# A hybrid attention layer pair on one core: the first query unit on the unscaled operand, r and bias applied to its results

## What is computed

```python
def rmsnorm(x, g):
    y = x * rsqrt(mean(x * x, axis=-1) + 1e-6)
    return y * g
h = rmsnorm(x, g[0])
proj = h @ w_in + b_in            # 256 x 2048 by 2048 x 2560
q, k, v = split(proj, [2048, 2304])
q = q * HEAD_DIM ** -0.5          # then 32 heads of 64; 4 heads of k and v
```

## Time and profile before

| | |
|---|---|
| median of 3 runs | 2267.7 us |
| the runs | 2261.79, 2267.7, 2271.3 us |
| the profiled execution | 2263.93 us, its span 2262.2 us |
| mean granted TensorE clock | 0.981 |
| TensorE busy | 2173.0 us, 96% of the span |
| VectorE busy | 1353.5 us, 60% |
| ScalarE busy | 1083.9 us, 48% |
| GpSimd busy | 249.2 us, 11% |

### The profile page before, as it was taken

One profiled execution on the slowest core, in us unless ns is written; L12 is line 12 of the kernel. 1 busy time (PEld: TensorE's weight loads), 2 busy tenths in 40 slices (PEclk: granted clock), 3 DMA queues, 4 the chain that ended last, 5 costly groups with the idle time before them and its releaser, 6 DMA issues.

```text
span 2262.2 us, 34176 instructions
## 1 busy us (share of the span) xinstructions
PE 2173.0 (96%) x11553; PEld 1805.5 (80%) x11553; DVE 1353.5 (60%) x2081; ACT 1083.9 (48%) x1639; POOL 249.2 (11%) x395
## 2 busy tenths in 40 slices
PE   8999989999999999998989998989999999999998
PEld 7777778888888888886776666768888888888886
DVE  7655567676767644445765444457766666664444
ACT  6766454444444443444455555445444444443443
POOL 3341000000000000003004554000000000000000
PEclk9999999999999999998999999999999999999999
DMA  6435545655565665553562222535555555665553
GB/s 211 136 116 177 177 139 170 202 182 194 174 201 178 192 208 191 186 188 110 189 222 66 74 74 81 172 129 186 187 184 193 178 195 176 197 209 189 186 187 129
DMA packets 107194, 381.12 MB, mean 168 GB/s; under 512 B 14114, under 2 KB 14578, under 8 KB 106482
## 3 DMA queue, kind: packets, MB, share of 16 engines
q1 hardware_dynamic: 104962, 373.69, 50.4%
q10 hardware_dynamic: 2160, 6.46, 0.7%
HBM read 377.97 MB, written 2.14 MB: 168 GB/s over the span
## 4 chain that ended last, share of the span: by engine, by line
PE 88%; DVE 6%; ACT 2%; issue 2%; POOL 1%; DMA 1%; DVEq 0%; ACTq 0%; POOLq 0%; SPq 0%
PE set L535 35%; PE set L603 29%; PE set L539 17%; DVE wlo L1266 2%; PE set L700 2%; PE set L682 1%; PE set L724 1%; PE set L627 1%; DVE scored L1524 1%; ACT whi L906 1%; DVE x_sb L1431 1%; POOL probs L490 1%; PE set L684 1%; DMA raw<-in_stream 0%; PE set L717 0%
## 5 line engine op out<-in xcount | busy, mean ns | idle before, releaser
L535 PE MATMUL set<-hs,whi 128*128 128x512 f32 x3584 | 1220.8, 403 | 20.4 <-DVE wlo L1266 7.6
L1266 DVE TENSOR_TENSOR wlo<-raw,whi 128x1024 fp32r<-128x1024 f32 x704 | 858.1, 1229 | 577.5 <-ACT whi L906 576.8
L906 ACT ACTIVATE whi<-raw 128x1024 fp32r<-128x1024 f32 x704 | 738.5, 1057 | 766.2 <-PE set L539 404.8
L539 PE MATMUL set<-hs,wlo 128*128 128x256 f32 x3584 | 856.2, 282 | 0.0
L539 PEld LDWEIGHTS set<-hs,wlo 128*128 128x128 f32 x3584 | 675.7, 191 | 78.6
L535 PEld LDWEIGHTS set<-hs,whi 128*128 128x128 f32 x3584 | 624.0, 191 | 119.4 <-issue 19.1
L603 PE MATMUL set<-whi,hid 128*128 128x512 f32 x1408 | 386.9, 395 | 0.0
L603 PEld LDWEIGHTS set<-whi,hid 128*128 128x128 f32 x1408 | 264.6, 188 | 63.5 <-DVE wlo L1266 0.6
L603 PE MATMUL set<-wlo,hid 128*128 128x512 f32 x704 | 222.5, 395 | 0.0
L603 PEld LDWEIGHTS set<-wlo,hid 128*128 128x128 f32 x704 | 132.4, 188 | 31.7
L603 PE MATMUL set<-whi,os 128*128 128x512 f32 x512 | 146.8, 400 | 0.0
(11 more groups left out here) (178 smaller groups left out, 1180.8 us busy)
## 6 DMA issues: line engine op xcount, KB each, us to landing
raw<-in_stream SPq DMA_DIRECT2D x704, 512.0 KB, 3.4
gain_rows<-rows ACTq DMA_DIRECT2D x4, 1024.0 KB, 5.2
xT<-in_x SPq DMA_DIRECT2D x8, 256.0 KB, 7.9
out_y<-out_f SPq DMA_DIRECT2D x3, 512.0 KB, 2.6
bo_rows<-rows ACTq DMA_DIRECT2D x1, 1024.0 KB, 7.9
wg_raw<-in_w_gates ACTq DMA_DIRECT2D x1, 768.0 KB, 4.4
out_y<-out_f SPq DMA_DIRECT2D x2, 256.0 KB, 2.4
w2k_sb<-in_w ACTq DMA_DIRECT2D x2, 128.0 KB, 5.2
```

Of the source, the lines that this page charges most:

```text
L535: return mm(sets[set_of(u)][:, t, 0:2 * w], whi[:, slot, cols], r, start=first, stop=final)
L539: return mm(sets[set_of(u)][:, t, w:2 * w], wlo[:, slot, cols], r[:, 0:w], start=False, stop=False)
L906: A(whi[:, slot, :], raw[:, slot, :], ACT.Copy).then_inc(hi_ready, 1)
L1266: V.tensor_tensor(wlo[:, slot, :], raw[:, slot, :], whi[:, slot, :].bitcast(F32), ALU.subtract).then_inc(lo_ready, 1)
```

## The change

KV0's chunks are no longer interrupted by `spread_r(0)`, which moves behind chunk 2 of Q0, uses a bank of set 1 instead of set 0 and waits for KV0's evacuation. Q0 reads the unscaled `hs`, and its results get the two-step treatment `q0_unscaled`: DVE adds the halves, DVE multiplies by r and by -1/8, ACT adds the bias. The scaling of `hs` starts in Q0's chunk loop (`scale_x(0)` at loop step c = 4, then one chunk for each step from 5 to 10) and ends behind Q0's evacuation (the low half of chunk 6, all of chunk 7). `high_of_scaled(c)` now waits for Q0's use of chunk c. The second query unit waits for all of it (`h_ready` of 16). `duplicate(0)` moves from DVE to ACT, with `ACT.Copy`. For chunk 0 of KV0, DVE makes `wlo` ahead of copying x out.

```diff
--- before.py
+++ after.py
...
@@ -632,19 +633,19 @@
                 def waits(c):
                     if c + 1 < CH:
                         turn_x(n, c + 1)
-                    if n == 0 and c == 6:
-                        spread_r(0)
                     pe.wait_ge(h_ready, h_before(n) + c + 1)
                 return waits
 
             def spread_r(n):
 
+                bank = sets[1] if n == 0 else norm_banks[n]
                 if n == 0:
                     pe.wait_ge(post_in, 32)
-                    nc.tensor.transpose(norm_banks[0][0:5 * KT, UT - 1, S:S + P], post_sb[:].rearrange("p a b -> p (a b)"),
+                    pe.wait_ge(evacuated, UT * (KV0 + 1))
+                    nc.tensor.transpose(bank[0:5 * KT, UT - 1, S:S + P], post_sb[:].rearrange("p a b -> p (a b)"),
                                         ident[:])
                 pe.wait_ge(diag_ready, n + 1)
-                mm(norm_banks[n][:, UT - 1, 0:S], ones[:], diag[:].rearrange("p a b -> p (a b)"), start=True,
+                mm(bank[:, UT - 1, 0:S], ones[:], diag[:].rearrange("p a b -> p (a b)"), start=True,
                    stop=True).then_inc(r_spread, 1)
 
             def attention(layer, u_q, g, last):
@@ -804,6 +805,8 @@
                            start=True, stop=True).then_inc(vc_rep_done, 1)
                     if layer == 1 and c == 0:
                         fold_halves(WV1)
+                    if layer == 0 and c == 2:
+                        spread_r(0)
                     if c != 5:
                         return
                     if layer == 0:
@@ -831,10 +834,6 @@
                     ins.then_inc(vc_done, 1)
                 return after
 
-            def scaled_waits(c):
-
-                pe.wait_ge(h_ready, CH + c + 1)
-
             for layer in range(2):
                 q0, o0, ff, dn = ((Q0, O0, FF0, DN0), (Q1, O1, FF1, DN1))[layer]
                 n = 2 * layer
@@ -850,13 +849,15 @@
                     unit(KW1, hs)
                     compress_unit(WK1, 0, after_wk)
                     compress_unit(WV1, 1, after_wv)
-                unit(q0, hs, waits=scaled_waits if layer == 0 else None, after_chunk=after_q0(layer))
+                unit(q0, hs, after_chunk=after_q0(layer))
                 if layer == 1:
 
                     pe.wait_ge(kc_ready, 1)
                     pe.wait_ge(vc_rep_ready, 1)
                     pe.wait_ge(gate_exp, 1)
                 pe.wait_ge(v_ready, 1 if layer == 0 else 3)
+                if layer == 0:
+                    pe.wait_ge(h_ready, 2 * CH)
                 with pe.Fori(0, GROUPS - 1) as g:
                     unit(q0 + 1, hs, lp=(g, CH, UT), tile_before=attention(layer, g * UT + UT * (q0 + 1), g, False))
 
@@ -980,8 +981,8 @@
             def high_of_scaled(c):
 
                 act.wait_ge(x_ready, c + 1)
-                act.wait_ge(chunk_used, first_chunk(KV0) + c + 1)
-                A(hs[:, c * CK:(c + 1) * CK, 0:S], half[:, 0, (c % 2) * CK:(c % 2 + 1) * CK, :],
+                act.wait_ge(chunk_used, first_chunk(Q0) + c + 1)
+                A(hs[:, c * CK:(c + 1) * CK, 0:S], half[:, 1, (c % 2) * CK:(c % 2 + 1) * CK, :],
                   ACT.Copy).then_inc(h_hi_ready, 1)
 
             def bias_kv(which):
@@ -1006,18 +1007,32 @@
                 take_root(0)
                 for c in range(RING - 1):
                     split(first_chunk(Q0) + c)
-                    high_of_scaled(c)
                 unit_first_half(KV0)
                 split(first_chunk(Q0) + RING - 1)
                 act.wait_ge(const_in, 16 * N_CONST)
-                high_of_scaled(RING - 1)
 
             def after_q0_split(c):
 
-                if RING <= c < CH:
-                    high_of_scaled(c)
+                if RING < c < CH + RING - 1:
+                    high_of_scaled(c - RING - 1)
                 if c in (RING + 1, RING + 2):
                     bias_kv(c - RING - 1)
+                if c == RING + 2:
+                    act.wait_ge(kv_biased, 2)
+                    for j in range(GROUPS):
+                        src = k_raw[(j % 2) * HD:(j % 2) * HD + HD, 0, j // 2, :]
+                        for h in range(2):
+                            ins = A(k_dup[h * HD:(h + 1) * HD, 0, j, :], src, ACT.Copy)
+                    ins.then_inc(k_dup_ready, 1)
+
+            def q0_unscaled():
+
+                unit_first_half(Q0, by_tile=True)
+                for t in range(UT):
+                    act.wait_ge(q0_scaled, t + 1)
+                    A(qg[:, t, :], qg[:, t, :], ACT.Identity, bias=b_q[:, t:t + 1]).then_inc(evacuated, 1)
+                for c in (CH - 2, CH - 1):
+                    high_of_scaled(c)
 
             def prenorm(n, gain, u):
 
@@ -1193,6 +1208,8 @@
                 def q0_evac():
                     if layer == 0:
                         act.wait_ge(prepared, 1)
+                        q0_unscaled()
+                        return
                     q_evac(q0)()
                     if layer == 1:
                         act.wait_ge(vc_rep_done, 1)
@@ -1339,14 +1356,14 @@
                     dve.wait_ge(h_ready, CH + c - 1)
                 for kt in range(CK):
                     k = c * CK + kt
-                    ins = V.scalar_tensor_tensor(half[:, 0, (c % 2) * CK + kt, :], xT[:, k, :], g_sb[:, 0, k:k + 1],
+                    ins = V.scalar_tensor_tensor(half[:, 1, (c % 2) * CK + kt, :], xT[:, k, :], g_sb[:, 0, k:k + 1],
                                                  rnorm[:], ALU.mult, ALU.mult)
                 ins.then_inc(x_ready, 1)
 
             def low_of_scaled(c):
 
                 dve.wait_ge(h_hi_ready, CH + c + 1)
-                V.tensor_tensor(hs[:, c * CK:(c + 1) * CK, S:2 * S], half[:, 0, (c % 2) * CK:(c % 2 + 1) * CK, :],
+                V.tensor_tensor(hs[:, c * CK:(c + 1) * CK, S:2 * S], half[:, 1, (c % 2) * CK:(c % 2 + 1) * CK, :],
                                 hs[:, c * CK:(c + 1) * CK, 0:S].bitcast(F32), ALU.subtract).then_inc(h_ready, 1)
 
             def first_norm():
@@ -1354,43 +1371,51 @@
                 dve.wait_ge(gains_in, 16)
                 for c in range(CH):
                     low_of_x(c)
-                    copy_x(c)
+                    if c > 0:
+                        copy_x(c)
                     split(c)
+                    if c == 0:
+                        copy_x(c)
                 token_r(sq_x, x_squared, 8, 0)
                 make_diag()
-                split(first_chunk(Q0))
-                spread_to_rnorm(0)
-                scale_x(0)
-                scale_x(1)
-                split(first_chunk(Q0) + 1)
-                low_of_scaled(0)
-                split(first_chunk(Q0) + 2)
-                scale_x(2)
-                low_of_scaled(1)
-                scale_x(3)
-                low_of_scaled(2)
-                scale_x(4)
+                for c in range(RING - 1):
+                    split(first_chunk(Q0) + c)
                 add_halves(KV0, lambda t: (k_raw if t < 2 else v_raw)[:, 0, t % 2, :])
                 split(first_chunk(Q0) + RING - 1)
-                low_of_scaled(3)
 
             def after_q0_split(c):
 
-                if RING <= c < CH:
-                    if c + 1 < CH:
-                        scale_x(c + 1)
-                    low_of_scaled(c)
                 if c == RING:
+                    spread_to_rnorm(0)
                     times_r(KV0, k_raw[:, 0], 1)
+                    scale_x(0)
+                if RING < c < CH + RING - 1:
+                    scale_x(c - RING)
+                    low_of_scaled(c - RING - 1)
                 if c == RING + 1:
                     times_r(KV0, v_raw[:, 0], 2)
                 if c == RING + 3:
                     dve.wait_ge(const_in, 16 * N_CONST)
                     V.tensor_scalar(b_q[:], b_in_sb[:, 0:16], -HD ** -0.5, None, ALU.mult).then_inc(o_read, 1)
                     V.tensor_scalar(neg_sinks[:], sinks_sb[:], -1.0, None, ALU.mult).then_inc(prepared, 1)
-                if c == RING + 4:
-                    dve.wait_ge(kv_biased, 2)
-                    duplicate(0)
+
+            def q0_unscaled():
+
+                def add(t):
+                    dve.wait_ge(half_ready, halves_before(Q0) + t + 1)
+                    V.tensor_tensor(half[:, 0, t, :], half[:, 0, t, :], sets[0][:, t, S:2 * S],
+                                    ALU.add).then_inc(q0_summed, 1)
+
+                add(0)
+                for t in range(UT):
+                    if t + 1 < UT:
+                        add(t + 1)
+                    dve.wait_ge(q0_summed, t + 1)
+                    V.scalar_tensor_tensor(qg[:, t, :], half[:, 0, t, :], -HD ** -0.5, rnorm[:],
+                                           ALU.mult, ALU.mult).then_inc(q0_scaled, 1)
+                low_of_scaled(CH - 2)
+                scale_x(CH - 1)
+                low_of_scaled(CH - 1)
 
             def row_of_r(tiles):
```

(6 more changed lines are left out.)

## The result

The changed kernel takes 2274.05 us (median of 20 runs, 2269.81 to 2280.7), the kernel before, run beside it, 2263.8 us (20 runs, 2260.15 to 2271.3). The ratio is 1.0046, 95% interval 1.0038 to 1.0054: **10.3 us slower**. The interval keeps it apart from zero, and it lies just under the 0.5% (11.3 us) from which the prediction would have called it slower. The forecast was 2275.5 us, against a median of 2267.7 shown for the kernel before; as a difference it was +7.8 us. The profiled execution spans 2273.7 us.

A forecast was written before the change was run, and what follows sets the result against it. TensorE, busy 96% of the span, was taken as the bound; a next unit 5.5 us later plus 2.3 us of slow clock gave +7.8 us on the median of 2267.7, so 2275.5 us, range 2268 to 2283.

The forecast's parts named there:

- KV0 and the spread: Head of layer 0, TensorE: KV0 ends at 35.5 us without the 3.3 us stall; spread inside Q0 takes 0.7 us.
- VectorE's wait for the spread: VectorE, during Q0: stands 3.2 us at the in-order wait for the spread, until r is there at 44.6 us.
- The key copies: ScalarE, during Q0: eight key copies at 0.30 us each, 2.4 us, upper bound 0.45 each; VectorE then idles 1.9 us.
- The evacuation: Behind Q0: its results in two steps take as long as in layer 1, 3.26 us, to 68.2 us.
- The serial tail: Behind Q0's evacuation: low and high halves and scaling of the last chunks run serially with hand-offs, 3.8 us, to 72.4.
- The restart: TensorE behind Q0: the next unit starts at 72.1 us in place of 66.57, 5.5 us later.
- The clock: TensorE behind the idle gap: restarts at 1.2 GHz for some 5 us, costing 2.3 us (1.3 to 3.0).
- rival 2: First woven unit, from 72 us: low clock outlasts the restart; with 15 us of it +13, 2281 us; chance 0.13.
- The sum: Head of layer 0: +5.5 us for the later next unit and +2.3 for the clock, +7.8 us, bounds +6.0 to +11.0.
- everything behind unchanged but for the shift: Sign of being right: behind the next unit's start and its slow clock, all only shifts, with no other change.
- Rival 1: Behind Q0: scaling mostly hidden under Q0, next unit at 60.8 us, 5.8 us earlier than before, total 2262; chance 0.07.
- Rival 3: KV0's chunks 6 and 7 wait for something else by up to 3 us: +10.8, 2278.5 us; chance 0.05.

The follow-up runs named there:

- e2: The changed kernel with the spread of r behind chunk 0 of Q0 instead of chunk 2: 2272.56 us in 6 runs, ratio 1.004.
- e3: The changed kernel with the next unit waiting for the scaled operand chunk by chunk instead of for all 16: ratio 1.0023.
- e4b: The changed kernel with TensorE's gap behind Q0 filled with 25 unused products: ratio 1.0044; restart to transpose 9.45 us in place of 11.45.
- e11: The changed kernel once more, unedited: 2277.57 us, ratio 1.0044 to the kernel before.
- e9: The kernel before, delayed by 22 unused products between Q0 and the next unit: ratio 1.0038.
- e10: The kernel before, delayed by 10 unused products between Q0 and the next unit: 2265.56 us in 12 runs against 2266.29, ratio 1.0000.
- e5: The changed kernel with the spread behind chunk 0, chunk-by-chunk waits and key copies two at a time over steps 6 to 9: 2270.24 us, ratio 1.002.
- e8: The kernel before, Q0 still scaled, with the spread behind KV0 and key copies on ScalarE two at a time: 2269.63 us, ratio 1.0009.

## Why the prediction was right, point by point

**KV0 and the spread.** The stall went as forecast. KV0 passes into Q0 near 35.3 us (forecast 35.5 less 0.25), and the spread starts at 43.86 (43.9). Its row lasts 0.6 us, but the next product of Q0 starts at 44.11, so it took 0.35 us of TensorE's time (forecast 0.7, lower bound 0.4). The low half of chunk 7 was in time (30.55).

**VectorE's wait for the spread** was 3.75 us against 3.2, and e2 showed that it counts in full: 3.5 us.

**The key copies** were mis-sized: 3.41 us in place of 2.4, 0.42 us each and one behind the other. The row they were sized by (0.30 each) was the far one; the upper bound of 0.45 was nearly met. It put 1 us on the chain: VectorE idled 2.73 us and not 1.9, and TensorE waited 0.43 us ahead of Q0's last chunk.

**The evacuation** took less than layer 1's 3.26 us: VectorE's eight instructions ran from 65.59 to 68.35, 2.8 us. In layer 1 two of its products took 0.55 and 0.93 us, and 0.42 here.

**The serial tail**, from VectorE's last product to the restart, took 4.5 us (68.35 to 72.85) against 4.2. e3 showed that it need not be waited for.

**The restart** came at 72.85 for 72.1, +6.3 us for +5.5. **The clock** cost 2.0 us by e4b, for 2.3; at 1.2 GHz TensorE ran for 4.5 us. In e11, the same kernel, it ran so for 3.5 us, at a cost of 1.6 us. The Trainium skill, TensorE: Matmul & The Clock Gate, section "Terms", puts the penalty of slow time at half of it at a clock of one half: an estimate of 2.25 us by that page for 4.5 us. The trace agrees within 0.3 us, and the profiles after an idle gap give 0.44, not 0.5, of the slow time. Of rival 2's "stuck" clock nothing was seen.

**The sum** of the head: +8.2 at the transpose, +8.4 at the norm, against +7.8 (in e11, +7.2 and +7.3, where the copy of x came 0.8 us earlier than before). The terms missed by up to 1 us each and partly cancelled: copies and tail too short, evacuation, spread and clock too long. **The step that failed** is the last: "everything behind unchanged but for the shift". It holds for the work, not for the time. The measured +10.3 us (8.6 to 12.2 by the interval) is 1.9 more than the head's in that profile, and e9, the kernel before with nearly the same delay (norm +8.0 us), had +0.38% (+8.6 us, 5 to 12.5), which fits both. Whether the changed kernel's 1.9 us come from more slow time behind the head or from scatter is open. That the time behind the head differs between kernels is shown by e10 and e5, by the totals and by the mean clock of their executions: 2.8 us in the head cost nothing, and a head 1.1 us shorter came out 4.5 us slower (ratio 1.002, 1.0005 to 1.0034).

That the total came within 1.5 us of the forecast 2275.5 is partly luck: its base, the median of three runs, was 3.9 us above the median of 20 runs of the same kernel, and the forecast difference was 2.5 us short.

Rival 1 (the tail hidden) did not happen: TensorE waited 13.2 us. Rival 3 did not occur. The chance of 0.26 for slower by over 0.5% was not far from the truth: the interval ends at 1.0054.

No edit tried here beat the kernel before. The nearest are e8 (1.0009, its interval holds 1) and e5 (1.002).

## What to carry to other kernels

Removing a stall from the busiest engine is worth what the next dependency lets through: find the time at which the chain of the other engines ends, and compare that, not the stall. A wait placed in an in-order queue (VectorE's for the spread) holds everything written behind it, so move the producer as far ahead of it as its data allow. When a change is worth less than 10 us in 2270, judge it by marks in the trace close to the edit, then ask whether the total can show it at all, and compare the mean granted clock of many executions before a cause is given for the rest.

## What the runs showed of the hardware that was not expected

ScalarE's copies of 64 x 256 from SBUF to SBUF did not overlap: 0.405 to 0.421 us each and 3.41 us for eight, while its copies of 128 x 256 out of PSUM took 1.19 us for four (63.12 in the timeline). That both sides lie in SBUF is not the reason: three high halves of weights, also SBUF to SBUF but 128 x 1024, took 2.94 us together at 1.05 each (from 32.44), so they overlapped. What the key copies have of their own is 64 partitions, with the output half changing from one to the next; no run here parts these two. The Trainium skill, ScalarE: Activation LUTs, section "What ACT_TABLE_LOAD costs", gives 186 ns plus 0.833 ns an element with immediate scale and bias, and an overlap of about 93 ns for instructions back to back, an estimate of 0.31 us each by that page: the row out of PSUM agrees (0.30), the key copies do not; they agree with the same figures without the overlap (an estimate of 0.40 us).

The granted clock of one and the same code behind the head differed from profile to profile, 65.3 to 102.9 us at 1.2 GHz, and with it the time by up to 13 us. Each us of it cost 0.44 us behind the idle gap of the head and 0.39 us in layer 1's projections and attention. A delay of 2.8 us ahead of it made no difference to the total (e10), and its 12 executions had 8 us less of slow time on average.
